# One decoder layer on eight cores: MLP by quarters with x1 in SBUF, weights cast into place, square roots batched

## The chip, the cores and the metric

The kernel is written for one Trainium2 chip and runs as one program on its 8 cores (cores 0 to 3 are one die, 4 to 7 the other). Each core has a matmul engine (TensorE, PE), a vector engine (DVE), an activation engine (ACT), a general one (POOL) and a sync engine (SP), which issues most DMAs. The metric is the device time in microseconds of the slowest core. Core r works on batch r//2 and on half r%2 of its 4096 tokens.

## What is computed

```
h = rmsnorm(x) * (1 + scale1) + shift1                   # x: 4 x 4096 x 1024, float32
x_rnn | y_rnn | u_pool | g_a | g_b = h @ W_in            # 1024 -> 5 * 1024
A = W_A( gelu(y_rnn) * RG_LRU(causal_conv4(x_rnn)) )     # gates are block diagonal, scan over tokens
B = W_B( scale * BlockLinear(trailing_mean(u_pool) - u_pool) )     # windows 2, 4, 8, 16
x = x + gate1 * W_out( sigmoid(g_a) * A + sigmoid(g_b) * B )
h = rmsnorm(x) * (1 + scale2) + shift2
x = x + gate2 * W_down( relu(h @ W_up)^2 )               # 1024 -> 4096 -> 1024
x = rmsnorm(x) * final_g
# shift, scale, gate: silu(c) @ W_ada + b, six vectors of 1024 for each batch
# RG_LRU: r, i = sigmoid(gates); log_a = -8 r softplus(a_param); h_t = a_t h_(t-1) + sqrt(1 - a_t^2) (i_t x_t)
```

## The kernel before

Weights are cast to bfloat16, matmuls accumulate in float32 in PSUM (8 banks of 128 x 512). Tiles are of 512 tokens. A core holds 2048 tokens of its own and a prefix of 2048 (zeros for the first half), over which only the state of the recurrence is carried on.

**Stages.** The start computes the first adaLN vectors with dot products on DVE (rows of `w_adaT` loaded by SP, `ada`) and loads `w_x`, `w_gb`, `w_bb` and others. Then tiles T=0 to 3 of the prefix, `lru(T)`, alternate with part B of the own tiles, `mix_b(m)` (w_u, pooling, w_gb, w_bb), whose result goes through the scratch `q_mb`; the normalised tiles go through the scratch `q_h`. `ada_late` computes the rest of the adaLN vectors in between: 32 loads of half a megabyte (`wTb`), each used in one dot product. Tiles T=4 to 7 are `lru(T, main=m)` and `mix_a(m)` with m = T-4. `lru` takes the eight column groups in four pairs; a pair is w_x matmuls, convolution on DVE (`xr`, copied to `xrb`), gate matmuls (w_gx, w_gr), Tanh, Exp, Square and Sqrt on ACT (`thi`, `thr`, `a`), a multiplication on POOL, two scans on DVE, and in the own tiles w_y matmuls, Gelu (`gel`) and the product `prodA`. `mix_a` has eight groups of w_ga and eight of w_aa over `prodA`, and puts `merged` together. Then comes the output projection (w_oo; x1 = x + gate1 times it), which writes x1 to the scratch `q_x1`, its norm, and the transposed `h2T` of all four tiles.

**The MLP** goes tile by tile: `up(m)` makes all 32 tiles `ff` of 128 columns (relu, square on ACT), `down(m)` has eight groups of 32 matmuls, each followed on DVE by `ps = ps * gtb2` and an addition to `x1r`, which is x1 read back. All of w_up and w_down is resident, 128 KB of each partition. Behind each pair of groups stand the last norm (ACT square, POOL statistics, DVE `SCALAR_TENSOR_TENSOR`) and the output.

**Casts.** POOL's DMA queue (q0) casts float32 to bfloat16; SP's is q1. w_y, w_ga, w_a and w_o, w_up and w_down are cast by 96 DMAs of 256 KB from DRAM to DRAM scratch (`q_wy`, ..., `q_dn`), and SP loads them from there when their place is free. `cast_some(2, ...)` puts two behind each of two gates of a pair from T=1 on: one gate is the copy to `xrb`, the other POOL's multiplication.

**The order** of all instructions is made by a planner on the host before the program is built (`Plan.order`): each step has an engine, an estimated time and a rank (stage), and the planner tries a few rules of priority and keeps the shortest plan of its own estimate. Each engine then runs its list in that order. The vectors gate1 and gate2 lie across partitions (`dv`, element c*128+p at partition p, column c) and reach all partitions as rows (`gtb`) by way of the scratch `q_g`:

```
N.add("sp", lambda e, ...: e.dma_start(out=q_g[gi].rearrange("(c p) -> p c", p=P), in_=DV(gv), ...), ...)
load(reg("gtb1", X1, 4 * K1), gtb1[:], q_g[0].partition_broadcast(P), 0.5, 7.0, reads=["qg0"])
```

Most instructions are recorded by helpers: L541 is ACT, L549 DVE, L556 POOL, L567 a matmul group, L535 a DMA. L645 and L1051 are transposes, L878 and L888 the pooling matmuls, L927 the DMA to `q_g`.

## Time and profile before

| | before |
|---|---|
| median of 3 runs | 1274.81 us (1256.88 to 1277.2) |
| the profiled execution | 1266.86 us |
| its span, slowest core (core 1) | 1265.3 us |
| spans of the cores | 1242.1 to 1265.3 us |
| TensorE matmuls | 1107.8 us busy (88%), 5256 |
| ACT | 693.1 us busy (55%), 1054 |
| DVE | 594.5 us busy (47%), 882 |
| POOL | 221.6 us busy (18%), 319 |
| q1 (SP's DMAs) | 120.18 MB, 33.1% of 16 engines |
| q0 (POOL's DMAs) | 35.46 MB, 26.5% of 16 engines |
| chain that ended last | PE 69%, DMA 12%, DVE 5%, ACT 5% |

Busy time is a mean over stages of different kinds, so the table alone doesn't tell where time is lost; that is read from windows of the trace, which give for a stretch how long each engine was busy, the mean granted clock of TensorE as a share of full speed, and how busy the 16 DMA engines were. Matmuls overlap: the mean of 379 ns that the page gives for one is longer than the distance between two, which is the length of a window over the number of matmuls in it.

### The profile page before, as it was taken

The page shows a single profiled execution, that of the slowest core. Times are in us where ns is not written, and L with a number is a line of the kernel's source. Part 1 is how long each engine was busy: PE and PEld are TensorE (multiplying, and loading weights), DVE is VectorE, ACT ScalarE, POOL GpSimd, SP SyncE. Part 2 cuts the span into 40 slices and gives each one's busy share as a digit, 9 for nine tenths or more (in the row PEclk, how much of TensorE's full clock was granted, in tenths as well). Part 3 has the DMA queues.
Part 4 walks back from the last instruction along what each step waited for, and adds up shares of the span by engine and source line. Part 5 has one row for each costly group of instructions (what it writes and reads, how often), then busy time and mean ns, then how long its engine had stood idle before and what let it go on. Part 6 is the DMA issues. An engine that isn't in the chain of part 4 may idle for free.

```text
span 1265.3 us, 16810 instructions; the slowest of 8 cores (1242.1 to 1265.3 us)
## 1 busy us (share of the span) xinstructions
PE 1107.8 (88%) x5256; PEld 506.0 (40%) x5256; DVE 594.5 (47%) x882; ACT 693.1 (55%) x1054; POOL 221.6 (18%) x319
## 2 busy tenths in 40 slices
PE   0367886588899998998989999999999999999993
PEld 0133432234354443443434444444444444444441
DVE  5583687645945747966676776401300220120022
ACT  0378895667658867483775844671164046116400
POOL 1521234143302213131220211000000000000000
PEclk9988998798899998887879999999999999999997
DMA  9999499997956999769942588740200200120120
GB/s 270 217 181 235 126 154 115 167 197 180 161 102 151 147 161 154 148 115 76 112 62 85 174 265 276 240 142 34 83 18 34 67 34 1 34 84 17 34 67 34
DMA packets 62071, 156.72 MB, mean 124 GB/s; under 512 B 7200, under 2 KB 22944, under 8 KB 59424
## 3 DMA queue, kind: packets, MB, share of 16 engines
q1 hardware_dynamic: 37184, 120.18, 33.1%
q0 software_dynamic: 24800, 35.46, 26.5%
q8 instruction: 44, 0.72, 0.3%
q14 instruction: 43, 0.35, 0.1%
HBM read 165.90 MB, written 50.34 MB: 171 GB/s over the span
## 4 chain that ended last, share of the span: by engine, by line
PE 69%; DMA 12%; DVE 5%; ACT 5%; issue 5%; SPq 2%; POOL 0%; DVEq 0%; ACTq 0%; POOLq 0%
PE ps L567 68%; DMA xt<-xin 5%; DMA q_mb<-mB 2%; DMA ada<-w_adaT 2%; DMA wTb<-w_adaT 2%; SPq L535 2%; DVE a L549 2%; DVE xr L549 1%; DMA h<-q_h 1%; PE ps L645 1%; ACT a L541 1%; ACT L541 1%; ACT xn L541 1%; ACT xr L541 1%; PE ps L1051 1%
## 5 line engine op out<-in xcount | busy, mean ns | idle before, releaser
L567 PE MATMUL ps<-h2T,wup 128*128 128x512 bf16 x1024 | 222.6, 379 | 0.3 <-ACT h2T L541 0.3
L567 PE MATMUL ps<-wdn,ff 128*128 128x512 bf16 x1024 | 221.7, 379 | 0.0
L549 DVE TENSOR_TENSOR ps<-ps,gtb 128x512 f32<-128x512 f32 x64 | 44.6, 698 | 366.7 <-PE ps L567 366.7
L549 DVE SCALAR_TENSOR_TENSOR xr<-ps,vecs,xr 128x511 f32<-128x511 f32 (+2 forms) x192 | 136.7, 743 | 39.8 <-ACT xr L541 35.0
L567 PEld LDWEIGHTS ps<-wdn,ff 128*128 128x128 bf16 x1024 | 100.2, 98 | 120.8
L567 PEld LDWEIGHTS ps<-h2T,wup 128*128 128x128 bf16 x1024 | 100.0, 98 | 120.3 <-issue 0.4
L541 ACT ACTIVATE junk<-x1r 128x1024 bf16<-128x1024 f32 x16 | 16.9, 1057 | 203.4 <-DVE x1r L549 203.4
L556 POOL TENSOR_SCALAR stat<-stat 128x1 f32<-128x1 f32 x65 | 15.9, 244 | 637.5 <-ACT junk L541 411.5
L556 POOL TENSOR_TENSOR thi<-thi,a 128x1024 f32<-128x1024 f32 x32 | 78.4, 2454 | 247.7 <-ACT a L541 183.1
L541 ACT ACTIVATE ps<-ps 128x512 f32<-128x512 f32 x128 | 74.8, 587 | 54.9 <-PE ps L567 54.8
L541 ACT ACT_TABLE_LOAD x70 | 89.8, 1283 | 24.6 <-PE ps L567 15.7
L549 DVE TENSOR_TENSOR_SCAN a<-thr,hst,thi 128x512 f32<-128x512 f32 x64 | 84.1, 1348 | 7.9 <-POOL thi L556 7.9
L645 PE MATMUL ps<-ident,xn 128*128 128x128 bf16 x264 | 25.4, 257 | 64.8 <-DVE dv L549 49.6
L541 ACT ACTIVATE ff<-ps 128x512 bf16<-128x512 f32 x128 | 76.0, 605 | 10.7 <-ACT ps L541 0.4
L567 PE MATMUL ps<-prodA,w_aa 128*128 128x512 bf16 x256 | 68.5, 426 | 7.3 <-ACT a L541 4.0
L541 ACT ACTIVATE xr<-ps,vecs 128x512 f32<-128x512 f32 x64 | 49.3, 781 | 35.9 <-PE ps L567 34.1
L567 PE MATMUL ps<-poolB,w_bb 128*128 128x512 bf16 x256 | 63.2, 400 | 5.0 <-ACT thb L541 3.8
L567 PE MATMUL ps<-hTp,w_x 128*128 128x512 bf16 x256 | 60.1, 391 | 7.8 <-ACT thi L541 5.7
L567 PE MATMUL ps<-xrb,w_gx 128*128 128x512 bf16 x128 | 40.0, 434 | 30.6 <-DVE xrb L549 20.4
L567 PE MATMUL ps<-h,w_x 128*128 128x512 bf16 x256 | 63.8, 408 | 1.9 <-DMA h<-q_h 1.9
L567 PE MATMUL ps<-h,w_y 128*128 128x512 bf16 x256 | 64.4, 408 | 0.4 <-ACT gel L541 0.4
L567 PE MATMUL ps<-h,w_ga 128*128 128x512 bf16 x256 | 64.6, 408 | 0.0
(117 smaller groups left out, 1486.1 us busy)
## 6 DMA issues: line engine op xcount, KB each, us to landing
wTb<-w_adaT SPq DMA_DIRECT2D x32, 512.0 KB, 13.8
xt<-xin SPq DMA_DIRECT2D x29, 512.0 KB, 10.3
ada<-w_adaT SPq DMA_DIRECT2D x16, 512.0 KB, 15.9
q_up<-w_up POOLq DMA_DIRECT2D x32, 256.0 KB, 13.1
q_dn<-w_dn POOLq DMA_DIRECT2D x32, 256.0 KB, 10.8
x1b<-xin SPq DMA_DIRECT2D x16, 512.0 KB, 5.6
q_x<-x1b SPq DMA_DIRECT2D x16, 512.0 KB, 9.0
wup<-q_up SPq DMA_DIRECT2D x8, 1024.0 KB, 14.1
```

The source lines that it names most:

```text
L535: return lambda e: e.dma_start(out=out, in_=in_)
L541: N.add("act", lambda e: e.activation(out=out() if callable(out) else out, in_=in_() if callable(in_) else in_, func=func, **kw), reads=re ...
L549: return m(**args)
L556: return m(**args)
L567: ins = e.matmul(ps[tok.bank][:, lo:hi], lhsT=l, rhs=r, start=(first and i == 0), stop=(last and i == n - 1))
L645: ins = e.transpose(out=psb[tok.bank][:, s * P:(s + 1) * P], in_=xn[:, s, c * P:(c + 1) * P], identity=ident[:])
L1051: ins = e.transpose(out=psb[tok.bank][:, s * P:(s + 1) * P], in_=xn2[:, s, c * P:(c + 1) * P], identity=ident[:])
```

## The change

- **MLP by quarters.** w_up's 4096 columns are taken in four quarters: `up(q, m)` makes 8 tiles `ff`, `down(q, m)` has eight groups of 8 matmuls (one quarter of the sum), and each is followed by the multiplication with `gtb2` and the addition to x1. So DVE has 128 such pairs, where it had 32. The last norm follows quarter 3.
- **x1 resident.** x1 stays in 16 tiles `x1_0` to `x1_15` in SBUF; `q_x1` is gone, with 16 writes and 16 reads.
- **Weights.** Quarter 0 is cast to scratch (8 casts of w_up, 8 of w_down) and loaded. Quarters 1 to 3 are cast by POOL's queue straight into the place of an earlier quarter: 12 DMAs, each half a weight quarter (1 MB of bfloat16). The casts are 48, and one stands behind each gate.
- **Square roots.** `lru` is written in two halves of two pairs, and the Sqrt of the first pair has a soft dependency (`mate`) on the Exp of the second.
- **q_g** is split on POOL in three bfloat16 parts, turned by three small matmuls, copied by ACT to `grow` (8 rows) and written by one DMA as 8 rows of 512 bytes.
- **Buffers.** `prodA` has two, `tha` four (`tt_` is gone), the late `ada_late` loads have one. 28 of its 32 steps now stand before T=4, 24 before. `junk1` is gone: the dot product is written in place.
- **The planner** no longer searches; it takes one rule of priority, shaken by six seeds (`HOW`), and the lead of several loads is set by new constants. All orders differ.

The diff, cut to its core:

```diff
+HOW = (2.0, 0, (2000001, 2000026, 2000034, 2000076, 2000106, 2000241))
 NRING = 34
+XLAG = 6.0
+BATCH = True
 DVE_PROD = True
-NADA = 24
-DVE_MG = True
+NADA = 28
+MBLAG = 3.0
+HLAG = 12.0
+MLAG = 10.0
...
-            casts += [(f"qup{qq}", k, q_up[qq, :, k, :], w_up[k * P:(k + 1) * P, qq * D:(qq + 1) * D]) for k in range(8)]
...
+        casts += [("qup", k, q_up[:, k, :], w_up[k * P:(k + 1) * P, 0:D]) for k in range(8)]
+        casts += [("qdn", k, q_dn[:, k, :], w_dn[k * P:(k + 1) * P, :]) for k in range(8)]
...
-                    cast_some(2, rc + 0.3, gk)
+                        cast_some(CASTS[T][pr % 2], rc + 0.3, gk)
...
+                    mate = [f"thr{(n + 1) % 3}_{j}" for j in range(2)] if pr % 2 == 0 and BATCH else []
+                    act(a2[:, :, :], thr[:, :, :], AF.Square, rk, ak, 1.06, rp)
+                    act(a2[:, :, :], a2[:, :, :], AF.Sqrt, ak, ak, 1.06, rp, soft=mate, table=("sqrt",), scale=-0.25, bias=0.25)
...
-                N.add("sp", lambda e, gi=gi, gv=gv: e.dma_start(out=q_g[gi].rearrange("(c p) -> p c", p=P), in_=DV(gv), allow_slow_non_contiguous=True), reads=[gk], writes=[f"qg{gi}"], us=0.1, rank=6.9, sem=f"qg{gi}", mb=0.1)
+                pool("copy", [gk], ["gsp0"], 0.3, 6.9, out=gsp[:, 0, :], in_=DV(gv))
+                pool("tt", [gk, "gsp0"], ["dvt0"], 0.3, 6.9, out=DV(DV_T0), in0=DV(gv), in1=gsp[:, 0, :], op=ALU.subtract)
+                pool("copy", ["dvt0"], ["gsp1"], 0.3, 6.9, out=gsp[:, 1, :], in_=DV(DV_T0))
+                pool("tt", ["dvt0", "gsp1"], ["dvt1"], 0.3, 6.9, out=DV(DV_T1), in0=DV(DV_T0), in1=gsp[:, 1, :], op=ALU.subtract)
+                pool("copy", ["dvt1"], ["gsp2"], 0.3, 6.9, out=gsp[:, 2, :], in_=DV(DV_T1))
+                tok = Bank(True)
+
+                def turn(e, tok=tok):
+                    ins = None
+                    for i in range(3):
+                        ins = e.matmul(ps[tok.bank][0:8, 0:P], lhsT=gsp[:, i, :], rhs=ident[:], start=(i == 0), stop=(i == 2))
+                    return ins
...
+        wof = [(D0, D1), (E0, U0), (D0, D1), (E0, U0)]
+        wup = [at(f"wup{q}", [P, 8, D], BF16, wof[q][0]) for q in range(4)]
+        wdn = [at(f"wdn{q}", [P, 8, D], BF16, wof[q][1]) for q in range(4)]
+        load(reg("wup0", D0, 16 * K1), wup[0][:], q_up, 2.0, 10.0, reads=[f"qup.{k}" for k in range(8)])
+        load(reg("wdn0", D1, 16 * K1), wdn[0][:], q_dn, 2.0, 10.5, reads=[f"qdn.{k}" for k in range(8)])
+
+        def quarter(q, rank):
             for h in range(2):
-                load(reg(f"wup{q}.{h}", upoff[q], 16 * K1), wup[q][:, :, h * 512:(h + 1) * 512], q_up[q, :, :, h * 512:(h + 1) * 512], 1.0, 10.0,
-                     reads=[f"qup{q}.{k}" for k in range(8)])
-        for q in range(2):
-            load(reg(f"wdn{q}", D0 + q * 16 * K1, 16 * K1), wdn[q][:], q_dn[q], 2.0, 10.5, reads=[f"qdn{q}.{k}" for k in range(8)])
-
-        for q in range(2, 4):
-            load(reg(f"wdn{q}", D0 + q * 16 * K1, 16 * K1), wdn[q][:], q_dn[q], 2.0, 10.5, reads=[f"qdn{q}.{k}" for k in range(8)])
+                hk_ = slice(4 * h, 4 * h + 4)
+                load(reg(f"wup{q}.{h}", wof[q][0], 16 * K1), wup[q][:, hk_, :], w_up[512 * h:512 * h + 512, q * D:(q + 1) * D].rearrange("(k p) n -> p k n", p=P), 2.0, rank, eng="pool")
+            for h in range(2):
+                hk_ = slice(4 * h, 4 * h + 4)
+                load(reg(f"wdn{q}.{h}", wof[q][1], 16 * K1), wdn[q][:, hk_, :], w_dn[q * D + 512 * h:q * D + 512 * h + 512, :].rearrange("(k p) n -> p k n", p=P), 2.0, rank + 0.1, eng="pool")
...
+            for j in range(8):
+                w = ff_no(q, m, j)
+                old = ["mBin"] if w < 8 else ["h2_1"] if w < 16 else [f"xn2_{(w - 16) // 2}"] if w < 24 else [f"mg3_{w - 24}"] if w < 32 else ["tha2"]
...
+            fk = [f"ff{ff_no(q, m, j)}" for j in range(8)]
+            wk = ["wdn0"] if q == 0 else [f"wdn{q}.0", f"wdn{q}.1"]
...
+                    group(tok, [(ff[ff_no(q, m, j)][:, s * P:(s + 1) * P], wdn[q][:, j, hs]) for j in range(8)], wk + fk, r)
...
+        for q in range(4):
+            for m in range(4):
+                up(q, m)
+                if m > 0:
+                    down(q, m - 1)
+            down(q, 3)
+            if q < 2:
+                quarter(q + 2, 25.0 + 4 * q)
+
+        N.emit(S, HOW)
```

What that makes of the order, at three places.

POOL's queue while the last prefix tiles run, from `lru(T)` and the statistics of the norms (`thi` is the multiplication behind whose gate casts stand; `stat` are statistics; a DMA row is a cast). Before:

```order
L535 DMA q_wy<-w_in 128x1024 x2
L556 TENSOR_TENSOR stat_45<-stat_45,expo_51 128x1
L556 TENSOR_TENSOR thi_53_95<-thi_53_95,a_58_100 128x1024
L535 DMA q_wga<-w_in 128x1024 x2
L535 DMA q_wa<-w_a 128x1024 x4
L556 TENSOR_TENSOR thi_54_96<-thi_54_96,a_59_101 128x1024
L535 DMA q_wga<-w_in 128x1024 x2
L556 TENSOR_SCALAR stat_45<-stat_45 128x1 x2
L556 TENSOR_TENSOR stat_45<-stat_45,expo_51 128x1 x2
L556 TENSOR_TENSOR thi_55_97<-thi_55_97,a_58_100 128x1024
L535 DMA q_wa<-w_a 128x1024 x2
```

and now:

```order
L568 TENSOR_TENSOR thi_55_97<-thi_55_97,a_59_101 128x1024
L547 DMA q_wy<-w_in 128x1024
L568 TENSOR_SCALAR stat_45<-stat_45 128x1
L547 DMA q_wga<-w_in 128x1024
L568 TENSOR_TENSOR stat_45<-stat_45,expo_51 128x1
L568 TENSOR_SCALAR stat_45<-stat_45 128x1
L568 TENSOR_TENSOR stat_45<-stat_45,expo_51 128x1
L568 TENSOR_SCALAR stat_45<-stat_45 128x1
L568 TENSOR_TENSOR stat_45<-stat_45,expo_51 128x1
L568 TENSOR_TENSOR thi_54_96<-thi_54_96,a_59_101 128x1024
L547 DMA q_wy<-w_in 128x1024
L547 DMA q_wga<-w_in 128x1024
```

Before, 12 casts stand in these 11 rows; now 4 in 12, one behind each gate.

TensorE between tiles m=1 and m=2 (`h_1` is the tile of m=1, `h_0` that of m=2; `w_aa` over `prodA` is the first group of m=1 that needs all its pairs; the numbers are those of buffers). Before:

```order
L567 MATMUL ps<-xrb_61_103,w_gr_84 128x512 x4
L567 MATMUL ps<-xrb_61_103,w_gx_83 128x512 x4
L567 MATMUL ps<-h_1_81_123,w_y_118 128x512 x16
L567 MATMUL ps<-h_1_81_123,w_ga_119 128x512 x16
L567 MATMUL ps<-h_0_80_122,w_x_82 128x512 x16
L567 MATMUL ps<-h_1_81_123,w_y_118 128x512 x16
L567 MATMUL ps<-h_0_80_122,w_x_82 128x512 x16
L567 MATMUL ps<-xrb_60_102,w_gx_83 128x512 x4
L567 MATMUL ps<-xrb_60_102,w_gr_84 128x512 x4
L567 MATMUL ps<-h_0_80_122,w_y_118 128x512 x8
L567 MATMUL ps<-prodA_105,w_aa_120 128x512 x16
```

and now:

```order
L579 MATMUL ps<-h_1_81_123,w_ga_119 128x512 x24
L579 MATMUL ps<-h_0_80_122,w_x_83 128x512 x24
L579 MATMUL ps<-h_1_81_123,w_y_118 128x512 x16
L579 MATMUL ps<-h_0_80_122,w_x_83 128x512 x8
L579 MATMUL ps<-h_1_81_123,w_ga_119 128x512 x8
L579 MATMUL ps<-xrb_62_104,w_gx_84 128x512 x4
L579 MATMUL ps<-xrb_62_104,w_gr_85 128x512 x4
L579 MATMUL ps<-h_0_80_122,w_y_118 128x512 x16
L579 MATMUL ps<-h_0_80_122,w_x_83 128x512 x16
L579 MATMUL ps<-xrb_61_103,w_gx_84 128x512 x4
L579 MATMUL ps<-xrb_61_103,w_gr_85 128x512 x4
L579 MATMUL ps<-prodA_92_134,w_aa_120 128x512 x16
```

Between the last `h_1,w_y` row and the first `w_aa` row there were 32 matmuls and are now 64; the gates and w_y groups of m=2 have come ahead of it.

DVE at the very end (`x1r` or `x` is x1; a pair is `ps<-ps,gtb` and the addition; `SCALAR_TENSOR_TENSOR` is the last norm). Before:

```order
L549 TENSOR_TENSOR ps<-ps,gtb_92_134 128x512
L549 TENSOR_TENSOR x1r_0_152_194<-ps,x1r_0_152_194 128x512
L549 TENSOR_TENSOR ps<-ps,gtb_92_134 128x512
L549 TENSOR_TENSOR x1r_0_152_194<-ps,x1r_0_152_194 128x512
L549 TENSOR_TENSOR ps<-ps,gtb_92_134 128x512
L549 TENSOR_TENSOR x1r_1_153_195<-ps,x1r_1_153_195 128x512
L549 TENSOR_TENSOR ps<-ps,gtb_92_134 128x512
L549 SCALAR_TENSOR_TENSOR x1r_0_152_194<-x1r_0_152_194,stat_45,fgb_152 128x1024
L549 TENSOR_TENSOR x1r_1_153_195<-ps,x1r_1_153_195 128x512
L549 SCALAR_TENSOR_TENSOR x1r_1_153_195<-x1r_1_153_195,stat_45,fgb_152 128x1024
```

and now:

```order
L561 TENSOR_TENSOR x_13_109_151<-ps,x_13_109_151 128x512
L561 TENSOR_TENSOR x_14_110_152<-ps,x_14_110_152 128x512
L561 SCALAR_TENSOR_TENSOR x_11_107_149<-x_11_107_149,stat_45,fgb_167 128x1024
L561 TENSOR_TENSOR ps<-ps,gtb_95_137 128x512 x2
L561 TENSOR_TENSOR x_14_110_152<-ps,x_14_110_152 128x512
L561 TENSOR_TENSOR x_15_111_153<-ps,x_15_111_153 128x512
L561 TENSOR_TENSOR ps<-ps,gtb_95_137 128x512
L561 SCALAR_TENSOR_TENSOR x_12_108_150<-x_12_108_150,stat_45,fgb_167 128x1024
L561 TENSOR_TENSOR x_15_111_153<-ps,x_15_111_153 128x512
L561 SCALAR_TENSOR_TENSOR x_13_109_151<-x_13_109_151,stat_45,fgb_167 128x1024
L561 SCALAR_TENSOR_TENSOR x_14_110_152<-x_14_110_152,stat_45,fgb_167 128x1024
L561 SCALAR_TENSOR_TENSOR x_15_111_153<-x_15_111_153,stat_45,fgb_167 128x1024
```

Before, the last norms of the last tile stand among pairs whose groups have 32 matmuls each; now the groups have 8, and four norms of the last rows stand at the end.

## Rows read from the trace of the kernel before

**Rows 1.** The page: engine rows, then groups of instructions (busy us, mean ns).
```profile
PE 1107.8 (88%) x5256; PEld 506.0 (40%) x5256; DVE 594.5 (47%) x882; ACT 693.1 (55%) x1054; POOL 221.6 (18%) x319
...
L567 PE MATMUL ps<-h2T,wup 128*128 128x512 bf16 x1024 | 222.6, 379 | 0.3 <-ACT h2T L541 0.3
...
L541 ACT ACT_TABLE_LOAD x70 | 89.8, 1283 | 24.6 <-PE ps L567 15.7
```

**Rows 2.** Windows of core 1: engines' busy us, granted clock, DMA share, GB/s.
```profile
core 1: us, PE busy (x) PEld busy (x) DVE busy (x) ACT busy (x) POOL busy (x), PEclk, DMA share, GB/s
160.00:360.00 200.00, 159.56 (x793) 72.79 (x792) 133.19 (x209) 140.15 (x207) 62.46 (x85) 0.89 0.98 164
200.00:240.00 40.00, 25.60 (x91) 9.56 (x88) 23.04 (x35) 22.75 (x33) 11.42 (x14) 0.84 1.02 121
360.00:400.00 40.00, 40.00 (x211) 19.12 (x210) 18.50 (x31) 24.03 (x37) 3.92 (x11) 1.00 0.47 122
600.00:640.00 40.00, 40.00 (x154) 16.57 (x153) 25.28 (x38) 30.27 (x41) 8.22 (x12) 0.81 0.88 112
1000.00:1040.00 40.00, 40.00 (x187) 18.16 (x186) 9.30 (x11) 12.69 (x22) 1.70 (x5) 1.00 0.20 66
```

**Rows 3.** Chain of waits, 150 to 300 us: start, us, what.
```profile
164.38 22.41 DMA wTb<-w_adaT
...
278.06 20.75 DMA xt<-xin
```

**Rows 4.** DMA queues and issues, 156 to 345 us (last column: us to landing).
```profile
q0 software_dynamic: 5184, 9.44, 49.3%
q1 hardware_dynamic: 7026, 20.60, 46.7%
...
xt<-xin SPq DMA_DIRECT2D x16, 512.0 KB, 16.5
```

**Rows 5.** DMA issues of the whole run (last column: median us to landing).
```profile
x1b<-xin SPq DMA_DIRECT2D x16, 512.0 KB, 5.6
...
w_gb<-w_in POOLq DMA_DIRECT2D x2, 1024.0 KB, 57.4
...
w_ga<-q_wga SPq DMA_DIRECT2D x1, 2048.0 KB, 25.6
```

**Rows 6.** Waits of TensorE, 470 to 680 us: in all, times, longest.
```profile
PE ps L567 <- ACT a L541: 4.0, 1, 4.0
PE ps L567 <- ACT thr L541: 3.3, 1, 3.3
```

**Rows 7.** Windows of 10 us around three waits (columns as in rows 2).
```profile
490.00:500.00 10.00, 4.01 (x11) 1.51 (x12) 7.87 (x10) 8.89 (x12) 1.03 (x2) 0.66 1.03 82
570.00:580.00 10.00, 6.05 (x19) 2.35 (x20) 8.04 (x13) 7.34 (x9) 0.14 (x1) 0.71 1.00 92
650.00:660.00 10.00, 6.70 (x18) 2.32 (x17) 8.57 (x12) 9.58 (x13) 0.04 (x1) 0.60 0.81 83
```

**Rows 8.** DMA packets and queue, 200 to 220 us.
```profile
DMA packets 1840, 1.96 MB, mean 98 GB/s; under 512 B 1111, under 2 KB 1111, under 8 KB 1839
...
q1 hardware_dynamic: 1268, 0.91, 33.4%
```

**Rows 9.** Timeline of the last 26 us (start, us, engine, what).
```profile
1239.74 4.05 PE L567 MATMUL ps<-wdn,ff 128*128 128x512 bf16 x18
...
1242.17 0.70 DVE L549 TENSOR_TENSOR ps<-ps,gtb 128x512 f32<-128x512 f32 x1 [0.23 <-PE ps L567]
...
1243.90 0.70 DVE L549 TENSOR_TENSOR ps<-ps,gtb 128x512 f32<-128x512 f32 x1 [0.16 <-PE ps L567]
...
1249.09 1.28 DVE L549 SCALAR_TENSOR_TENSOR x1r<-x1r,stat,fgb 128x1024 f32<-128x1024 f32 x1 [2.63 <-POOL stat L556]
```

**Rows 10.** Cores: span and mean granted clock.
```profile
core 1: 1265.3 us, clock 0.935
...
core 3: 1264.0 us, clock 0.950
```

More of the change, by code:

```diff
@@ L997, in mix_a @@
[L997 to L1001 removed]
+                group(tok2, [(w_aa[:, k, c * P:(c + 1) * P], prodA[m % 2][:, k, :]) for k in range(8)], ["wa"] + [f"pA{m % 2}_{k}" for k in range(8)], r)
```

339 lines of the change are left out of this document (168 added, 171 removed).

## The prediction

> **What bounds the kernel now.** I read the page's engine rows first: TensorE is busy for 88% of the span and no other engine for more than 55% [rows 1], so the question is where TensorE is not at full pace. The MLP is not such a place. Its up and down matmuls are 2048 of the 5256 [rows 1], and a stretch inside it shows 187 matmuls in 40 us at a granted clock of 1.00, 0.214 us each, with TensorE busy all the time [rows 2]. Whatever the change does to the MLP can only cost time there, or nothing.
>
> The stretch 160 to 360 us is another matter. TensorE is busy 159.6 of 200 us, at a mean clock of 0.89, and the DMA engines are full (0.98) [rows 2]. In 200 to 240 it does 91 matmuls where 360 to 400 shows 211, with the DMA share down to 0.47 and the clock at 1.00. So some 40 us of idle time and, from the clock, about 0.11 x 160 = 18 us lie in this stretch: 58 us is all that it can give.
>
> The chain of waits says what holds it: between 164 and 299 us it is mostly landings, and the five longest come to 101.8 us (two of them are shown) [rows 3]. These are DMAs of half a megabyte or less. In the stretch such an `xt` load lands in 16.5 us (median of 16) [rows 4], while `x1b`, of the same source and size but issued when the queues are nearly empty, needs 5.6 [rows 5]. What fills the engines is the cast queue q0, 49.3% of them against 46.7% for q1, which carries every load that the chain waits for [rows 4].
>
> The next place is the tiles T=4 to 7. TensorE waits 4.0 us for `a` (at 573.95) and 3.3 us for `thr` (at 654.34), each time before the first w_aa group of a tile [rows 6]. In the 10 us around those points TensorE issues 19 and 18 matmuls, and 11 around a third (495.99, for xrb), at clocks of 0.71, 0.60 and 0.66; the plain pace there is 154 in 40 us, 38.5 in 10 [rows 2, 7].
>
> **Casts, 160 to 345 us.** The window holds 36 casts, 9.44 MB, for 49.3% of 189 us = 93 us of the sixteen engines, 2.59 us a cast [rows 4]. Now one cast follows each gate, not two, and the wup and wdn casts fall from 64 to 16; over the same TensorE work the order of POOL's queue holds 18 casts. That frees 46.6 us of DMA time. Against it four more `wTb` loads move here, 0.5 MB each; at q1's rate in the window (20.60 MB for 88 us, 4.3 us a MB) they are 2.1 us each, 8.5 in all. Upper bound, if the stretch is limited by transfer alone: 46.6 - 8.5 = 38 us, or 42 without the added loads. Lower bound, if the loads are only issued too late: 5 us. I take it by the chain: 101.8 us of landings, in engines that have 46.6/189 = 25% less to do, become 25 us shorter. **-25 (-42 to -5).**
>
> The Trainium skill (DMA: Bandwidth & Descriptors, Queues, rings and completion order) says that each DMA engine goes round between the queue rows that have work, a packet at a time. The equal shares of q0 and q1 agree with it. By it a load is relieved only while q0 is empty, which would now be half of the time, and then wholly: the landings would fall by 101.8 x 0.5 x (1 - 5.6/16.5) = 34 us, and the sum would be 1225 in place of 1234. The text goes on with 25.
>
> **q_g in 8 rows.** Before, 1024 packets of 4 bytes are written twice. In 200 to 220, with 1111 packets under 512 B, q1 moves 0.91 MB [rows 8] where its mean in the window is 20.60 x 20/189 = 2.18. The 1.27 MB not moved are 12 us of that queue. The first one stands in the stretch; the second comes much later, and nothing in the chain waits for it. With the chain already relieved by the casts I take half. The six tiny POOL operations, three matmuls and one copy that replace it come to under 2 us on engines that wait. **-6 (-12 to 0).**
>
> **T=4 to 7.** `prodA` gets a second buffer, `tha` four, and the order is another one. Before, 32 matmuls stand between the last w_y group of m=1 (`h_1`) and its first w_aa, now 64: at 0.214 us the work that covers the gap grows from 6.8 to 13.7 us. For m=2, counted in the same way, it grows from 8.5 to 26.3 us. The chain from the last w_y (gelu, two scans, `prodA`) is what the 4.0 and 3.3 us waited for. Matmuls missing against 38.5 in 10 us: 19.5, 20.5 and 27.5, at 0.26 us 5.1, 5.3 and 7.1. The first two should go; of the third (the xrb behind two scans), which the change doesn't address, half. **-14 (-21 to 0).** If the new order puts an equal wait elsewhere, this is 0.
>
> **Square roots batched.** The mate makes the Sqrt of an even pair wait for the Exp of the next, so that two share one table load. In the order ACT has 3 loads fewer than before, 3 x 1.28 = 4 us [rows 1], on an engine busy 55%. **0.** So this part does next to nothing of what it says: the order had most of the batching already.
>
> **x1 resident.** 16 writes to q_x1 and 16 reads go; they ran beside the matmuls of the output projection and the MLP, where TensorE is busy all the time (the MLP's DMA share is 0.20 [rows 2]). **0.**
>
> **MLP by quarters.** DVE's pair (ps times gtb2, add to x1) comes once for 8 matmuls and not once for 32: 128 pairs. Back to back a pair starts every 1.73 us (1242.17 to 1243.90) [rows 9], and 8 matmuls last 1.71 us; an up of 64 matmuls without such pairs stands beside each down, so DVE needs at most half of the time. **0**; without that cover 128 x 0.02 = 3 us. Weights: a load of two halves of a weight moves 2 MB of bf16, 8 casts' worth, 8 x 2.59 = 20.7 us. Matmuls between the place coming free and the first use: 120 for wup3 (25.7 us), 264 for wdn2, some 500 or more for the others but wup1, whose issue stands 41.9 us ahead. All fit. **0 (0 to +8)**, 8 if wup3 comes a third slower.
>
> **Loads with less lead.** w_ga is now issued 12.0 us of TensorE work before its first use, before it was 25.6, just its landing [rows 5], under full queues. With the casts thinner I take a landing of 16. **+4 (0 to +12).** wup0 leads its first use by 47 us and waits for 8 casts of q_up that are issued late now: **+1 (0 to +8).** The startup issues its `ada` loads in another order and the w_x loads behind later ones, and 28 instead of 24 dot products of 1.3 us stand on DVE before T=4: **+3 (-3 to +12).**
>
> **Tail.** The last matmul ends at 1243.8 and the last stt starts at 1249.09 and ends 6.6 us later than that matmul [rows 9]. Now the last 16 groups are all down (27.4 us), and DVE has 16 pairs and 8 stt of 1.28 in them: 16 x 1.6 + 8 x 1.28 = 35.8 us. It ends some 10 us behind: **+4 (+2 to +8).**
>
> **Sum:** -25 - 6 - 14 + 4 + 1 + 3 + 4 = -33. The profiled execution took 1266.9 us (span 1265.3), so 1234. That execution is 0.6% under the median of 1274.8; I forecast 1234, not scaled.
>
> **Rivals.**
> A. The DMA engines are full, but what holds TensorE in the stretch is the order: a load can be issued only when its buffer is free, and SP waits in line. Then 5 us come from the casts, 3 from q_g and half of 14 from T=4 to 7, against +12 of costs: 1264; with half of the cast term 1256. For it: DVE is busy 133 of the 200 us [rows 2]. Against: the longest pieces are landings, not DVE. 1250 to 1272, about 1256. Chance 0.22.
> B. The weight loads of the quarters don't get through. The nearest rows of a load from float32 into bf16 in SBUF are w_gb's two halves, landed 57.4 us after issue (2 MB together, at startup, all queues full) [rows 5]. At that price wup3 is late by 57.4 - 25.7 = 32 us and wup1 by 15: 1234 + 47 = 1281, slower than before. It decides from 41 us of lateness, loads of about 54 us. Against: in the MLP the DMA share is 0.2. Chance 0.05.
> C. The granted clock. On core 1, 600 to 640 shows 154 matmuls at 0.81, while the MLP has 187 at 1.00 [rows 2]; a matmul costs 0.046 us more. If the MLP, now with twice the changes between up and down, ran at that level, all 2048 would cost 94 us, and 1435 of them are enough to pass 1300. Rows against it: before, 0.81 came behind waits in T=4 on, and the MLP stayed at 1.00. Chance 0.05. The Trainium skill (TensorE: Matmul & The Clock Gate, Part 1) states that a die's clock falls to 13/16 once three of its cores run dense matmuls. This trace disagrees: with the same dense matmuls on all eight cores the MLP shows 1.00.
>    The clock can also not explain a gain by itself: core 3 kept a mean of 0.950 against core 1's 0.935 and still took 1264.0 [rows 10].
> D. More of it than I count: the stretch is limited by transfer alone (-38), q_g gives 12 and all of T=4 to 7 21: 1234 - 13 - 6 - 7 = 1208, and less with no costs. Chance 0.12.
>
> **How the numbers follow.** Forecast case, 1215 to 1250: 0.56, nearly all of it faster. From what a measurement here can tell, 2% is 25.5 us: faster is under 1249.3, slower over 1300.3. Faster: 0.54 + 0.12 = 0.66. Same: 0.02 + 0.22 + 0.04 = 0.28. Slower: C and a hundredth of the rest, 0.06. The range takes in the forecast's own, most of A up to 1262, and D down to 1206.
>
> **What would show it.** In the profile after: a stretch 160 to 345 us with fewer q0 packets, `xt` landing near 12 us and TensorE busy over 85%; no wait of 3 us before a w_aa group; no 4-byte packets; MLP matmuls at 0.214 us without a wait for wup or wdn; the last stt some 10 us behind the last matmul. I am wrong if `xt` lands faster and TensorE waits as long, for DVE or for other loads (A), or if waits for wup appear (B), or if the MLP shows 154 matmuls in 40 us (C).

## The result, and the profile after

The changed kernel took **1211.21 us** (median of 4 executions, 1209.63 to 1215.16); the kernel before took 1266.2 beside it (4 executions: 1256.88, 1257.59, 1274.81 and 1277.2; why they fall in two pairs is told with e11_qg2nd). The ratio is 0.9594, with a 95% interval of 0.9494 to 0.9694: faster, by about 55 us. The forecast was 1234 with a range of 1206 to 1262, and "faster" at 0.66. So the sign was right and the time in the range, but the gain (57 us from the profiled execution of before, where 33 were forecast) is 1.7 times the one worked out. In a few executions of the experiments below the cores of one die, or two of them, had a low mean clock (down to 0.80 on all four, in one of 1437 us) and took longer; they are left out of the times unless the text names them.

The profiled execution took 1209.6 us (span 1208.1, on core 3). From its page come the engine rows, two queues and some groups of instructions. These answer to [rows 1]:

```profile
PE 1071.7 (89%) x5262; PEld 495.0 (41%) x5262; DVE 730.5 (60%) x1074; ACT 687.1 (57%) x1054; POOL 215.0 (18%) x293
...
q1 hardware_dynamic: 21920, 90.82, 24.4%
q0 software_dynamic: 24224, 35.46, 22.2%
...
L561 DVE TENSOR_TENSOR ps<-ps,gtb 128x512 f32<-128x512 f32 x160 | 111.3, 697 | 228.6 <-PE ps L579 228.3
L579 PE MATMUL ps<-h2T,wup 128*128 128x512 bf16 x1024 | 224.1, 379 | 0.7 <-ACT h2T L553 0.6
...
L553 ACT ACTIVATE ps<-ps 128x512 f32<-128x512 f32 x128 | 74.1, 585 | 219.9 <-PE ps L579 219.1
...
L553 ACT ACT_TABLE_LOAD x68 | 87.2, 1283 | 33.1 <-PE ps L579 22.8
```

TensorE is busy 36 us less, with 6 matmuls more (those that turn q_g), and DVE 136 us more, with 96 more of the MLP's pairs. The up matmuls of the MLP cost what they did, 224.1 us against 222.6. The windows of core 3 answer to [rows 2] (columns: stretch, length, busy us of each engine with the number of instructions, granted clock, DMA share, GB/s):

```profile
160.00:360.00 200.00, 180.54 (x991) 85.85 (x990) 149.02 (x235) 151.75 (x229) 56.97 (x77) 0.97 0.71 156
200.00:240.00 40.00, 32.92 (x169) 14.90 (x168) 31.58 (x48) 31.07 (x48) 11.56 (x21) 0.96 0.93 201
480.00:680.00 200.00, 194.79 (x898) 86.86 (x897) 164.62 (x223) 150.42 (x206) 42.30 (x42) 1.00 0.41 105
1000.00:1040.00 40.00, 40.00 (x187) 18.19 (x186) 9.70 (x16) 18.87 (x32) 0.00 (x0) 1.00 0.00 1
```

In 160 to 360 us TensorE now does 991 matmuls where it did 793, and in 200 to 240 it does 169 where it did 91. The MLP stretch at the bottom is as before: 187 matmuls at clock 1.00. The queues and issues of 156 to 345 us, also of core 3, answer to [rows 4]:

```profile
q1 hardware_dynamic: 6942, 23.71, 46.1%
q0 software_dynamic: 2592, 4.72, 24.7%
...
xt<-xin SPq DMA_DIRECT2D x18, 512.0 KB, 7.0
wTb<-w_adaT SPq DMA_DIRECT2D x17, 512.0 KB, 7.6
```

The casts' queue has half its packets and half its share, as counted; the `xt` load lands in 7.0 us where it took 16.5 on core 1 (on core 3 itself it took 11.5 before).

A total tells little about where time went, so I worked out one more table from the traces. The work of TensorE is measured in us at full clock (columns divided by 2400). For each core I take the time at which N us of it are done, less N: that is the **lag**, all that this core's TensorE has lost so far to waits and to the clock. Each entry is the median over the eight cores. In the traces, cores 2 and 4 lack about 100 of the 5256 or 5262 matmul records, so that their lags read up to 21 us too high; medians over the other six differ from the entries of before and after by less than 2 us at every N. The bulk of T=4 to 7 lies between N=340 and 500 (its first w_aa group starts near 329 before and 344 after, its first w_y group near 290 and 264), the output projection and the MLP behind 500. "End" is the end of the last matmul less 1022, "rest" what is left of the span from there.

```
N              1    60   110   120   190   340   500   end   rest
before        50    88   112   142   158   175   202   209    22
after         55   101   109   113   127   148   156   165    18
e1_qg32       51    88   110   121   148   166   187   197    22
e2_thin       51    89   112   125   135   155   217   226    21
e3_both       51    89   111   119   130   150   176   186    21
e4_cast2x     55   102   122   132   153   190   198   203    19
e5_qg4        56   104   112   128   142   164   175   183    18
e8_oldplan    47    90   105   106   121   133   159   166    17
e9_splice190  47    91   106   108   122   143   151   157    18
e10_splice330 47    91   106   107   122   147   160   163    18
e0_after      55   103   111   117   133   156   164   167    18
e11_qg2nd     51    89   112   147   162   181   203   213    22
```

From before to after, the lag up to N=60 grows by 13 us; between 60 and 190 it is 44 less (70 then, 26 now); 190 to 340, 4 more; 340 to 500, 19 less (27, 8); the MLP 2 more; the rest 4 less. That is 48 us in the median core. The span of the slowest core fell by 57.2 (1265.3 to 1208.1): before, three cores stood 12 us over the median of 1252 (two of them in [rows 10]), after, the slowest stood 4 us over it. e0_after is the changed kernel once more, run with the experiments; from one trace of it to the other an entry moves by up to 8 us, so differences of a few us between rows say little.

### The profile page after: what moved, and what is told of

It is laid out like the page before. It is cut to its first block, busy times and chain, and to the rows that moved or that the text cites. A ratio compares the mean times of both kernels' runs of the same rounds, so it can differ in the third digit from the quotient of the medians.

```text
span 1208.1 us, 17046 instructions; the slowest of 8 cores (1191.9 to 1208.1 us)
## 1 busy us (share of the span) xinstructions
PE 1071.7 (89%) x5262; PEld 495.0 (41%) x5262; DVE 730.5 (60%) x1074; ACT 687.1 (57%) x1054; POOL 215.0 (18%) x293
## 4 chain that ended last, share of the span: by engine, by line
PE 76%; DMA 7%; issue 5%; ACT 4%; DVE 4%; POOL 1%; SPq 0%; DVEq 0%; ACTq 0%; POOLq 0%
PE ps L579 75%; DMA wpl<-w_pl 3%; DMA ada<-w_adaT 1%; DMA w_ga<-q_wga 1%; DVE a L561 1%; DVE xr L561 1%; DMA xt<-xin 1%; ACT a L553 1%; ACT poolB L553 1%; PE ps L657 1%; PE ps L1084 0%; SPq L547 0%; PE ps L907 0%; ACT L553 0%; ACT thr L553 0%
## 5 line engine op out<-in xcount | busy, mean ns | idle before, releaser
L561 DVE TENSOR_TENSOR ps<-ps,gtb 128x512 f32<-128x512 f32 x160 | 111.3, 697 | 228.6 <-PE ps L579 228.3
L579 PE MATMUL ps<-h2T,wup 128*128 128x512 bf16 x1024 | 224.1, 379 | 0.7 <-ACT h2T L553 0.6
L561 DVE TENSOR_TENSOR x<-ps,x 128x512 f32<-128x512 f32 x160 | 109.6, 690 | 14.1 <-DVE ps L561 1.2
L561 DVE TENSOR_TENSOR_SCAN a<-thr,hst,thi 128x512 f32<-128x512 f32 x64 | 81.3, 1301 | 18.0 <-POOL thi L568 17.8
L568 POOL TENSOR_SCALAR stat<-stat 128x1 f32<-128x1 f32 x65 | 23.5, 362 | 348.0 <-ACT junk L553 203.1
L579 PE MATMUL ps<-h,w_ga 128*128 128x512 bf16 x256 | 58.9, 385 | 4.8 <-DMA w_ga<-q_wga 4.8
L579 PE MATMUL ps<-w_u,hTm 128*128 128x512 bf16 x256 | 57.9, 386 | 5.6 <-ACT hTm L553 5.6
L579 PE MATMUL ps<-hTm,w_gb 128*128 128x512 bf16 x256 | 60.4, 385 | 0.9 <-ACT thr L553 0.7
L579 PE MATMUL ps<-poolB,w_bb 128*128 128x512 bf16 x256 | 58.2, 379 | 1.3 <-ACT poolB L553 1.3
L579 PE MATMUL ps<-h,w_y 128*128 128x512 bf16 x256 | 57.9, 379 | 0.0
L579 PE MATMUL ps<-h,w_x 128*128 128x512 bf16 x256 | 57.7, 379 | 0.0
## 6 DMA issues: line engine op xcount, KB each, us to landing
wup<-w_up POOLq DMA_DIRECT2D x6, 1024.0 KB, 16.8
wdn<-w_dn POOLq DMA_DIRECT2D x6, 1024.0 KB, 14.3
```

The source lines that it names most:

```text
L561: return m(**args)
L568: return m(**args)
L579: ins = e.matmul(ps[tok.bank][:, lo:hi], lhsT=l, rhs=r, start=(first and i == 0), stop=(last and i == n - 1))
```

## The experiments

The theories. **C**: the casts crowd the loads, and thinning them brings most of the gain. **G**: the write of `q_g` in 4-byte pieces costs far more than the 6 us I gave it. **O**: it is the new order, in T=4 to 7 and elsewhere. **S**: something is lost again at the start. Each group of kernels ran beside its own executions of the kernel before, on one chip for each group: median 1283.77 us for e1, e2, e3 and e5, 1279.6 for e0, e4, e7 and e8, 1281.13 for e6, e9 and e10, 1278.3 for e11. So kernels of different groups are best compared by their ratio to the kernel before.

### The casts and q_g, each alone in the kernel before

**e1_qg32** writes q_g as 128 rows of 32 bytes, and changes nothing else:

```diff
-N.add("sp", lambda e, gi=gi, gv=gv: e.dma_start(out=q_g[gi].rearrange("(c p) -> p c", p=P), in_=DV(gv), allow_slow_non_contiguous=True), ...)
+N.add("sp", lambda e, gi=gi, gv=gv: e.dma_start(out=q_g[gi].rearrange("(p c) -> p c", p=P), in_=DV(gv)), ...)
```

> The kernel before, with its order of instructions as it is; only the two DMAs to q_g are written as 128 rows of 32 bytes each and not as 1024 elements of 4 bytes (this permutes the gate vectors, so the output isn't the layer's). Casts theory (the prediction): the cast queue is what slows the loads, q_g costs 6: 0 to 12 us less than before. Rival Q (formed from the two traces: TensorE loses 20 to 34 us at one place, right behind the first q_g write): the 4-byte packets hold up the loads and q_mb writes, 20 to 30 us less. Order theory: under 5 us.

Measured: 1245.03 us, ratio 0.9695 (0.9679 to 0.9710), 39 us less. This one line brings more than half of what the whole change brings. In the lag table the largest step is at one place, N=110 to 120 (30 us lost before, 11 now), where loads land behind the first write [rows 3]; half of those 19 us are lost again by N=190, and 12 remain at the end of the median core. The longest link of the chain that the forecast had put down to the casts lies there: it is the store of q_mb on core 1, 19 us behind q_g's write in the same queue,

```profile
209.69 26.93 DMA q_mb<-mB
```

and in e1_qg32, with all casts as they were, the same store lands in 18.3 us (core 3: 20.6, where it took 37.1). The second write is the one of which I said that nothing in the chain waits for it. That was the chain of core 1. The chain of waits of core 3, before, 575 to 660 us (start, us, what), reads:

```profile
574.89 6.22 PE ps L567 x24
...
582.16 27.99 DMA q_g<-dv
...
610.73 21.05 DMA h<-q_h
...
632.01 5.02 PE ps L567 x16
```

And the waits of SP's own queue, 560 to 660 us of the same core (what was waited for: us in total, times, longest):

```profile
SPq L157 <- DMA q_g<-dv: 26.8, 1, 26.8
```

SP's queue is in order. It comes to the load of `gtb2`, which reads q_g, and stands 26.8 us until 4 KB have landed; `h` for T=7, which needs nothing of it, is issued only then. With rows of 32 bytes the same wait is 12.0 us, in profile e1_qg32 of core 3:

```profile
SPq L157 <- DMA q_g<-dv: 12.0, 1, 12.0
```

In the profiled execution of before, TensorE then waits for `h` on three of the eight cores (3, 4 and 6: 11.2, 4.2 and 0.8 us). So G points to two places of different kind: loads and stores of the same queue crawl, and later an in-order queue stands still. How the 39 us fall on the two is told with e11_qg2nd.

**e2_thin** thins the casts alone: one behind each gate up to T=3, three from T=4 on. One line of its edit holds it (`g` is the gate, `n` the casts already met behind it):

```diff
...
+                for _ in range((1 if n == 0 else 0) if int(g[4:]) <= 32 else (2 if n == 0 else 1)):
...
```

> The kernel before, same order on all engines, but POOL's queue issues one cast behind a gate up to T=3 and three behind a gate from T=4 on; all 96 are made. Casts theory: the stretch 160 to 345 us becomes about 25 us shorter (5 to 42), some of it given back in T=4 to 7 where casts are denser: 15 to 25 us less than before. Rival Q: 5 to 10 us less, since the place behind q_g stays. Order theory: under 5 us.

Measured: 1275.26 us, ratio 0.9933 (0.9915 to 0.9951), 8.5 us less. Windows of core 0, e2_thin:

```profile
160.00:360.00 200.00, 171.90 (x917) 79.65 (x917) 148.14 (x238) 149.41 (x221) 64.58 (x79) 0.94 0.75 144
480.00:680.00 200.00, 146.88 (x631) 63.16 (x630) 124.52 (x173) 110.07 (x149) 51.61 (x61) 0.85 0.99 115
```

The first row is the forecast's mechanism: 917 matmuls, where the same core did 776 before. The lag at N=190 is 23 us less (135 for 158), close to the term of 25; on top of e1_qg32, where no 4-byte write stands in the way, the same edit (e3_both) brings 18 (130 for 148). The second row is the price: the casts that were put off fill the DMA engines (0.99) in T=4 to 7, where this core did 718 matmuls before and does 631 now. There 35 us more than before are lost, and the median core's last matmul ends 17 us later than in the profile of before. The link of core 3 above is now on all eight cores: SP's queue stands 44.7 to 49.1 us for the second write of q_g, and TensorE waits 29.2 to 34.5 us for `h`. Core 0, 560 to 690 us:

```profile
SPq L157 <- DMA q_g<-dv: 46.5, 1, 46.5
...
PE ps L589 <- DMA h<-q_h: 31.2, 1, 31.2
```

C holds where it was priced, but to put casts off is no gain in itself; the change has 16 wup and wdn casts left where before has 64.

**e3_both** makes both edits in the kernel before.

> Both edits of e1_qg32 and e2_thin in the kernel before. Casts theory: 25 to 31 us less. Rival Q: 30 to 35 us less, hardly more than e1_qg32 alone. Order theory: under 8 us less, so that nearly all of the gain in the stretch (some 40 us in the trace) is the new order's.

Measured: 1237.51 us, ratio 0.9632 (0.9614 to 0.9649), 46 us less. The times add up (39 + 8.5), but not by one mechanism: on top of e1_qg32 the thinner casts take 11 us off the median core's last matmul (197 to 186), alone they put 17 on it. In T=4 to 7 e3_both loses 26 us (its TensorE waits at most 7.7 us for `h`) and e2_thin 62, so with the old writes of q_g the casts that were put off meet the second write. What the change has beyond e3_both comes to some 17 us by the ratios and 22 by the times, and by the table it lies in T=4 to 7 (26 there, against 8 in the changed kernel) and in 60 to 190 (41 against 26), less 12 at the start.

### The changed kernel, with one thing put back

**e5_qg4** is the changed kernel with the old write of q_g:

```diff
-N.add("sp", dma_fn(q_g[gi].rearrange("(c p) -> c p", p=P), grow[:]), reads=["grow"], ...)
+N.add("sp", lambda e, gi=gi, gv=gv: e.dma_start(out=q_g[gi].rearrange("(c p) -> p c", p=P), in_=DV(gv), allow_slow_non_contiguous=True), reads=["grow", gk], ...)
```

> The changed kernel with all its steps and its order, but q_g is written again as 1024 packets of 4 bytes from the vector across partitions. Casts theory: 6 us slower than the changed kernel (0 to 12), about 1217. Rival Q: 20 us or more slower, 1231 or more. Order theory: no change, 1211.

Measured: 1227.49 us, ratio 0.9557 (0.9534 to 0.9581).

**e0_after** is the changed kernel as it is, on the chip of the next four.

> The changed kernel itself, beside the kernel before on the same chip as the other experiments, so that e5_qg4 (ratio 0.956) has its partner. Casts theory: e5_qg4 costs 6 us, so 0.951. Rival Q: it costs 20 us or more, so 0.940 or less. Order theory: 0.956.

Measured: 1216.09 and 1214.76 us, where the kernel before took 1276 to 1285 us; the ratio of the medians is 0.950 (with two executions, no interval is on record), and the whole change brings 64 us here. So the 4-byte writes cost 12 us in the changed order by the times of two chips, and 7 by the ratios (0.956 against 0.950, where the casts theory had 0.951), but 39 in the old order. The same two DMAs are three times dearer or more where the queue behind them is full and what waits in it is needed at once: at N=110 to 120 e5_qg4 loses 16 us and before lost 30. The second write stands in nobody's way there: in e5_qg4 it is issued at 617.4 us on core 3 and both `gtb` loads behind it, while the last `h` went out at 588.9; in the order of before the load of `gtb2` and the wait for q_g come ahead of the last `h`. Behind N=340 e5_qg4 loses some 4 us more than the changed kernel.

**e4_cast2x** issues each of the 48 small casts twice, the second into a scratch tensor that nobody reads:

```diff
+                if sem in TWICE:
+                    S.dma(eng, self.again[i], "again", [], [f"again{i}"], [])
```

> The changed kernel with all its steps in its order; behind each of its 48 casts POOL's queue issues the same cast once more, into a scratch that nobody reads, so that the cast traffic is doubled. Casts theory: about the relief of the forecast is given back, 25 us slower than the changed kernel (5 to 42). Rival Q (q_g was the hindrance, casts matter little, as e2_thin's 8 us say): 3 to 10 us slower.

Measured: 1248.29 and 1244.01 us, ratio 0.9726 (0.9641 to 0.9810): 31 us more than the changed kernel beside it. This is theory C from the other side, and it comes out near the 25 us: by N=190 the lag is 26 us more. The profiled execution was a longer one (1263.0 us, with cores 0 and 1 at a mean clock of 0.935). Core 1 shows for 156 to 345 us:

```profile
q0 software_dynamic: 5051, 9.21, 43.3%
q1 hardware_dynamic: 6519, 22.61, 39.0%
...
xt<-xin SPq DMA_DIRECT2D x18, 512.0 KB, 6.6
wTb<-w_adaT SPq DMA_DIRECT2D x17, 512.0 KB, 11.7
```

The `xt` load, on which I hung the term, still lands in 6.6 us under nearly as many casts as before. `wTb` takes 11.7 us for 7.6, and TensorE waits for the result of casts: for w_ga 10.9 to 15.9 us on the eight cores, where in the changed kernel it waits 0 to 4.8. Core 3, 160 to 520 us of e4_cast2x:

```profile
PE ps L584 <- DMA w_ga<-q_wga: 15.2, 1, 15.2
```

How the rest of the 31 us falls on `wTb` and others is not shown. The size of the term was right. Its witness, `xt`, moved with the casts in the order of before (e2_thin, core 1: 6.5 us for 16.5) and not in this one.

**e6_nobatch** takes the square roots' batching away (`BATCH = False`).

> The changed kernel without the soft dependency that makes the Sqrt of a pair wait for the Exp of the next (BATCH off); the planner's rule and seeds are the same, but its plan shifts with it. Forecast: the batching is worth 0, the time stays within 6 us of the changed kernel (about 1215 on these chips). Rival: the table loads (1.28 us each) are on the path of a pair to the scans, 8 us or more slower.

Measured: 1215.37 us, ratio 0.9488 (0.9443 to 0.9534), where the changed kernel has 0.950. ACT has 77 table loads here for 68, 9 more or 11.5 us, and no time is lost by them. The part named in the change's own title is worth nothing here that a measurement can tell.

**e8_oldplan** keeps all steps of the changed kernel and gives them the old, searching planner:

```diff
-    def order(self, tilt=10.0, rounds=1, shakes=(), hop=0.15, dma_gbps=0.28, keep=1, swap=8.0):
+    def order(self, hop=0.15, dma_gbps=0.28, keep=1, tilts=(2.0, 5.0, 10.0), swap=8.0, rounds=4):
```

> The changed kernel's steps, buffers, casts and q_g, with the order made by the planner of the kernel before (its search over three tilts and four rounds). Order theory: much of the gain is the new order's, 15 us or more slower than the changed kernel. Rival Q: what the order does is small beside q_g; within 8 us of it.

Measured: 1212.14, 1208.28 and 1224.32 us, ratio 0.9482 (0.9366 to 0.9598), which can't be told from the changed kernel (in the third execution cores 0 and 1 stand 15 us over the rest, at a mean clock of 0.95). But the same sum has other parts: the start is 11 us better (lag 90 at N=60, for 101), and T=4 to 7 loses 26 us, as e3_both does, where the new order loses 8. So the second `prodA` and the four `tha` don't remove those waits by themselves; the new order does, and pays for it at the start. That is O and S at once, read from one trace of each.

### The start

**e7_start** puts SP's first 22 loads back in the order of the kernel before:

```diff
+        start = ["srow"] + [f"ada{j}" for j in range(12)] + [f"xs{j}" for j in range(4)] + ["vecs"] + [f"ada{j}" for j in range(12, 16)]
```

> The changed kernel with SP's first 22 loads in the order of the kernel before: ada 0 to 11, xs, vecs, ada 12 to 15; all else in its order. The two traces show the changed kernel 13 us behind at the same TensorE work when the start is over. Theory S: DVE takes the dot products in the order 0 to 15 while SP issues 0, 8, 7, 5, 1, 4, 11, 2 ..., so DVE and the w_x loads behind acc11 and acc5 come late; 8 to 13 us faster than the changed kernel. Rival: POOL's order of loads and the later matmuls of w_u hold the start, 0 to 3 us.

Measured: 1216.26, 1218.18 and 1221.54 us, ratio 0.9511 (0.9452 to 0.9571): no gain. The edit was a bad one. The waits of DVE in the first 62 us, of e7_start, then of the changed kernel:

```profile
DVE dv L565 <- DMA vecs<-vecs: 17.2, 1, 17.2
...
DVE junk L565 <- DMA ada<-w_adaT: 1.1, 3, 0.5
```

```profile
DVE junk L561 <- DMA ada<-w_adaT: 10.5, 3, 6.3
```

The wait for `ada` went, as meant. But `vecs` fell from 14th to 18th of the loads, and DVE's order, which was not changed with it, wants it early. So e7_start shows only that the order of the loads and that of the engine have to fit. S was left to the next two.

**e9_splice190** and **e10_splice330** take the old planner's order up to 190 (330) us of TensorE's planned work, and the new one for the rest. The PSUM banks are dealt anew.

```diff
+        one, two = self.order_search(), self.order(*how)
...
+            if pe > work:
+                break
```

> The changed kernel's steps in a spliced order: up to about 190 us of TensorE's planned work the order of e8_oldplan (the searched plan), behind it the changed kernel's own order. The trace of e8_oldplan is 10 us ahead of the changed kernel at that point and loses it again in T=4 to 7. If the two places are independent: 8 to 12 us faster than the changed kernel, about 1205. If the start's lead is only borrowed (loads that come due later all the same): within 3 us of it.

> As e9_splice190, but with the searched order up to about 330 us of TensorE's planned work, which is just ahead of the place where it loses 26 us and the changed kernel 7. Independent places: 15 to 20 us faster than the changed kernel, about 1197. Borrowed lead: within 3 us of it.

e9_splice190 measured 1202.61 us (1200.79 to 1203.89), ratio 0.9393 (0.9355 to 0.9431), the best version: 13 us below e6_nobatch, which is as fast as the changed kernel and ran beside it. It has the old start (91 at N=60) and the new T=4 to 7 (8 us), so S is shown, at 10 us. e10_splice330 should have been its equal and took 1224.32 us, ratio 0.9564 (0.9505 to 0.9622), though in the median its last matmul ends within 6 us of that of e9. Its cores:

```profile
core 0: 1221.9 us, clock 0.946
core 1: 1221.4 us, clock 0.950
core 2: 1202.8 us, clock 0.970
```

Then 540 to 580 us of e10_splice330, core 0 and below it core 2:

```profile
540.00:580.00 40.00, 40.00 (x154) 16.54 (x152) 33.00 (x44) 26.75 (x37) 10.30 (x9) 0.81 0.33 39
```

```profile
540.00:580.00 40.00, 38.41 (x176) 17.32 (x178) 32.02 (x43) 31.82 (x45) 8.46 (x12) 1.00 0.35 60
```

Core 0 never waits here and does 154 matmuls for core 2's 176. From 460 to 590 us cores 0 and 1 show 0.81 and 495 matmuls each, cores 2 and 3 show 0.99 and more. Six cores end at 1200 to 1204, and the time is that of the pair. In each of its four executions one pair of neighbours, or two, stands so (mean clock 0.946 to 0.954), in e9_splice190 none does. I have no cause for it.

### The second write of q_g alone

**e11_qg2nd** gives only the second of the two writes its rows of 32 bytes, in the kernel before.

> The kernel before, but only the second write to q_g (row gate2, near 584 us) goes as 128 rows of 32 bytes; the first, near 191 us, keeps its 1024 elements of 4 bytes (this permutes one gate vector). The two together are worth 39 us (e1_qg32, ratio 0.970). The forecast's step: the first holds up the loads of the stretch, the second holds nothing: 0 to 3 us less than before. Rival H, from the chain of waits on core 3 of the kernel before (q_g 28.0 us, then h<-q_h 21.1 us behind it in SP's queue, then TensorE): the second holds up the tile of T=7 and is worth more than the first, 20 to 28 us less than before.

Measured: 1259.9, 1282.22 and 1279.54 us, where before took 1278.3: by the time alone nothing is settled. The spans of the single cores tell more. In the last two of these executions the slowest cores are one pair, at a mean clock of 0.927 to 0.933, and they stand 18 to 21 us over all others. I set cores under 0.937 aside, in every kernel alike, and put the spans of the rest together:

```
kernel                      executions, cores   spans, us
before, beside e1_qg32      6, 48               27 at 1237 to 1264, 21 at 1268 to 1285
before, beside e11_qg2nd    4, 26               17 at 1247 to 1265,  9 at 1267 to 1275
e11_qg2nd                   4, 24               all at 1248 to 1260
e1_qg32                     5, 36               all at 1234 to 1244
```

In the kernel before a core has two ways to go, some 22 us apart in the medians (1257 and 1280 in the first row, 1251 and 1273 in the second; the edges of the second row's two groups are only 2 us apart), and with eight cores the slowest goes the longer one in every such execution here. Beside the result itself two of the four did not: 1256.88 and 1257.59. Without the second 4-byte write none of 24 cores does. So this write makes some 15 to 23 us of the 39, on some four cores in ten, and the first, which every core feels, the other 16 to 24 (medians 1256 in e11_qg2nd and 1240 in e1_qg32, on different chips). The `h` link above is the likely form of the longer way, but that is argued: no trace is kept of a core of before that went it, and on core 3 TensorE waits only 11.2 us of that link's 21.05. In e2_thin, where all eight wait 29 to 35 us, all 32 cores end at 1265 to 1275. A lower clock is the rival: cores of the longer way have a mean of 0.943, of the shorter 0.949, and by an estimate from TensorE's 1108 us that is at most 7 of the 22 us. What sends a core the longer way, in one execution and not in the next, was not tried. In the lag table, a median over cores of one execution, this hardly shows: in T=4 to 7 e11_qg2nd loses 22 us, before 27.

## Why the prediction was right, and where it was not

**The bound was read rightly.** 160 to 360 us and T=4 to 7 were named as the two places, the MLP as one where nothing is to be won. The 48 us of the median core are 44 + 19 in these two places and 4 at the tail, less 13, 4 and 2 elsewhere. That is one attribution of several: measured alone in the old order, q_g brings 39 and the casts 8.5 us, and the rest some 20.

**Casts, forecast -25.** e2_thin's 23 at N=190 (18 without the 4-byte writes) and e4_cast2x's 26 there confirm the size. The witness failed: I asked for `xt` near 12 us and it took 7.0. The Trainium skill (DMA: Bandwidth & Descriptors, Queues, rings and completion order) states that the engines go round between the queues that have work. By that rule a load is relieved wholly while q0 is empty, which gave 34 us and a total of 1225. By it `xt` would land in 11.1 us on the average of 16.5 and 5.6, by my proportion in 12.4; the 7.0 us is under both, and nearer to the rule by little. But e4_cast2x, with q0's share at 43.3% and `xt` at 6.6, agrees with neither, so no run here shows that the rule sized the gain.

**q_g, forecast -6.** This is the step that failed. The argument was the bytes that one queue did not move in 20 us, 12 us, halved; and "the second comes much later, and nothing in the chain waits for it". The runs show 39 us in the order of before, 16 to 24 for the first write and 15 to 23 for the second, and 7 to 12 for both in that of after. Two things were missed. I had read the chain of one core, and on core 3 the second write is a link of 27.99 us, followed by one of 21.05. And I priced a queue by the bytes that it didn't move, not by the instructions that stand in line behind one that waits. Rival A had the words for it ("SP waits in line"), but took them for a reason to expect less. And the longest of the landings that I gave to the casts, the 26.93 us of q_mb, stood behind q_g's write: it falls to 18.3 with that write alone changed. Thus e3_both, which has just the two edits of these two terms (31 us), gained 46, and e1_qg32 alone more than the whole forecast.

**T=4 to 7, forecast -14.** Measured -19 from N=340 on, -18 from N=290. The cause that I gave, more matmuls over the gap, is supported by e8_oldplan: with the same buffers and the old order these tiles still lose 26 us. The waits of TensorE in 470 to 680 us of the changed kernel answer to [rows 6]:

```profile
PE ps L579 <- DVE xrb L561: 6.2, 5, 2.4
PE ps L579 <- DVE tha L561: 0.6, 1, 0.6
PE ps L579 <- ACT gel L553: 0.6, 1, 0.6
```

No wait of 3 us before a w_aa group is left, and xrb costs 6.2 us in five pieces, where half a third piece was expected to stay. Part of the gain is the clock: 1.00 on all cores from 500 to 650 us. On core 1, on which the forecast was made, more of it is: from N=340 to 500 cores 0 and 1 lost 39 us before, cores 5 to 7 19 to 22, and cores 0 and 1 alone stood at 0.81, from 520 to 640 us but for one wait. The forecast saw the 0.81 [rows 2] and had no term for its absence.

**Start, forecast +3 (-3 to +12).** It was +13 at N=60, just outside: 5 up to the first matmul, 8 behind it. DVE waits 10.5 us for `ada`, and TensorE waits for the weights that the order issues late (core 3, first 160 us):

```profile
PE ps L579 <- DMA wpl<-w_pl: 5.2, 1, 5.2
```

I had named both reorderings and priced them at next to nothing. e9_splice190 takes 10 of the 13 us back.

**w_ga, forecast +4.** One wait, 4.8 us, at 458 us of the changed kernel's core 3, which is ahead of N=340; it lies in the part of the table that loses 4 us more than before. Over the eight cores it is 0 to 4.8. Right, by the one step that rested on a single lead and a single landing.

```profile
PE ps L579 <- DMA w_ga<-q_wga: 4.8, 1, 4.8
```

**MLP, x1, square roots, forecast 0.** The MLP's waits, from 700 us on, are all in two rows of core 3:

```profile
PE ps L579 <- ACT h2T L553: 0.6, 1, 0.6
PE ps L1084 <- DVE x L561: 0.3, 1, 0.3
```

So neither the weight loads of the quarters (rival B) nor the clock (rival C) came. The loads landed in 16.8 us (wup) and 14.3 (wdn), where 57.4 at startup [rows 5] was the upper bound. DVE's 96 more pairs held nothing up there. No run has the quarters or the resident x1 alone; the table has 7 us lost behind N=500 before and 9 after. Table loads fell by 2, not 3, and e6_nobatch shows that 9 more cost nothing.

**Tail, forecast +4.** Timeline of the changed kernel, core 3, which answers to [rows 9]:

```profile
1183.65 6.42 PE L579 MATMUL ps<-wdn,ff 128*128 128x512 bf16 x29
...
1193.34 2.47 DVE L561 SCALAR_TENSOR_TENSOR x<-x,stat,fgb 128x1024 f32<-128x1024 f32 x2
...
1196.79 1.28 DVE L561 SCALAR_TENSOR_TENSOR x<-x,stat,fgb 128x1024 f32<-128x1024 f32 x1 [0.98 <-POOL stat L568]
```

The last matmul ends at 1190.07 and the last stt at 1198.1, 8.0 us behind it where 6.6 was the distance before: +1.4, not +4 (and this though the forecast reckoned a pair at 1.6 us, where its own rows have 1.73). From there to the end of the span it is 10.0 us now and 14.9 before, so the tail as a whole is 4 us shorter. Of SP's waits at the very end, this row is the last one, before and then after:

```profile
SPq L500 <- PEq L500: 11.4, 1, 11.4
```

```profile
SPq L511 <- PEq L511: 6.6, 1, 6.6
```

Why the engines finish sooner was not tried.

**The sum** held through errors of both signs. In the median core the two places of gain gave 63 us where 45 were forecast, the start cost 10 more, the tail 8 less. That the range held is in part luck: q_g was worth six times its term in the order that the forecast read it from, and the 0.81 on its core, behind the 17 to 20 us that it lost there over cores 5 to 7, had no term. And a forecast made on one core leaves out how far the slowest stands over the middle: of the 57 us of span 9 are that. Rival D, with 1208 us at 0.12, is the case nearest to the result; its q_g term of 12 is the upper of the two figures (7 and 12) that e5_qg4 gives in the changed order, and its transfer term of 38 was not tested apart.

## What to carry to other kernels

Price a DMA by who stands behind it in its in-order queue and by its number of pieces, not by its bytes: two writes of 4 KB, in 1024 pieces each, cost this kernel 39 us in its old order. Read the chain of waits on more than one core, since the slowest core is not always held by the same link. And when a new order wins in one part of a program and loses in another, cut the two together: the splice at 190 us took the better half of each, and was the fastest kernel measured.
